# Stream products of an attention step in 32-column weight blocks, and the stream values by token rows

## What is computed

```python
def dsa_attend(q, qi, wi, k_all, v_all, ki_all, q_pos, k_pos, top_k):
    s_idx = jnp.einsum('bthd,bsd->bths', qi, ki_all)
    score = jnp.einsum('bths,bth->bts', jax.nn.relu(s_idx), wi) * IDX_SCALE
    score = jnp.where(adm[None], score, NEG)          # chunk-causal
    _, idx = lax.top_k(score, top_k)
    ...
    logits = jnp.einsum('bthd,btkhd->bhtk', q, k_sel) * (HEAD_DIM ** -0.5)
    p = jax.nn.softmax(jnp.where(valid[:, None], logits, NEG), axis=-1)
    return jnp.einsum('bhtk,btkhd->bthd', p, v_sel)
```

## Time and profile before

| | |
|---|---|
| Time, median of 3 runs | 2992.81 us (2989.2 to 2993.98) |
| The profiled execution's own time | 2993.22 us |
| Its span, first to last instruction | 2991.4 us |
| TensorE matmul busy | 2916.6 us, 97% |
| TensorE weight load busy | 2874.6 us, 96% |
| VectorE, ScalarE, GpSimd busy | 46%, 34%, 33% |
| DMA | 238.8 MB, 80 GB/s |
| Mean granted TensorE clock | 0.987 of full speed |

### The profile page before, as it was taken

The page is one execution under the profiler, slowest core; times in us unless marked ns, Lnnn a source line. Parts: engine busy times, 40 slices in busy tenths (PEclk is TensorE's granted clock), DMA queues, the critical chain, the costliest instruction groups (busy, mean ns, idle before and its releaser), DMA issues.

```text
span 2991.4 us, 50397 instructions
## 1 busy us (share of the span) xinstructions
PE 2916.6 (97%) x19500; PEld 2874.6 (96%) x19516; DVE 1361.3 (46%) x1857; ACT 1012.5 (34%) x1431; POOL 997.1 (33%) x468
## 2 busy tenths in 40 slices
PE   8999999999999999999999999999989999999997
PEld 8999999988899999999999999999889999999997
DVE  4324246777533532424532333568674334324245
ACT  5312225536432342212343222254463323412223
POOL 2333333241233333333333333333312333333332
PEclk9999999999999999999999999999999999999998
DMA  3222222232122222222222222222321222222222
GB/s 116 77 78 70 84 77 85 77 116 92 59 70 77 71 77 75 73 84 71 84 71 73 75 77 77 79 84 84 117 86 59 77 74 74 70 78 77 77 77 91
DMA packets 73073, 238.80 MB, mean 80 GB/s; under 512 B 8336, under 2 KB 16784, under 8 KB 72464
## 3 DMA queue, kind: packets, MB, share of 16 engines
q1 hardware_dynamic: 58464, 210.00, 20.6%
q10 hardware_dynamic: 14512, 27.51, 2.6%
HBM read 229.22 MB, written 8.27 MB: 79 GB/s over the span
## 4 chain that ended last, share of the span: by engine, by line
issue 58%; PE 26%; POOL 13%; POOLq 1%; DVE 1%; ACT 1%; ACTq 0%; DVEq 0%
PE lin L404 22%; POOL w_lo L339 12%; PE bank L404 2%; POOLq L379 0%; POOL tmp L370 0%; PE bank L565 0%; PE bank L550 0%; POOLq L337 0%; POOL tmp L376 0%; PE lin L565 0%; PE bank L527 0%; POOLq L392 0%; PE lin L527 0%; DVE x L1479 0%; PE bank L575 0%
## 5 line engine op out<-in xcount | busy, mean ns | idle before, releaser
L339 POOL TENSOR_TENSOR w_lo<-w_raw,w_hi 128x1024 fp32r<-128x1024 f32 x392 | 948.3, 2419 | 1951.7 <-ACT w_hi L706 1940.2
L404 PE MATMUL lin<-h_hi,w_hi 128*128 128x320 f32 x4064 | 939.6, 313 | 18.8 <-DVE h_lo L1048 12.1
L404 PE MATMUL lin<-h_lo,w_hi 128*128 128x320 f32 x4064 | 931.3, 311 | 0.0
L404 PE MATMUL lin<-h_hi,w_lo 128*128 128x320 f32 x4064 | 930.5, 310 | 0.0
L706 ACT ACTIVATE w_hi<-w_raw 128x1024 fp32r<-128x1024 f32 x392 | 415.4, 1060 | 1508.0 <-PE lin L404 1380.6
L404 PEld LDWEIGHTS lin<-h_hi,w_hi 128*128 128x128 f32 x4064 | 684.2, 189 | 25.9 <-DVE h_lo L1048 12.9
L404 PEld LDWEIGHTS lin<-h_lo,w_hi 128*128 128x128 f32 x4064 | 683.8, 189 | 0.0
L404 PEld LDWEIGHTS lin<-h_hi,w_lo 128*128 128x128 f32 x4064 | 683.5, 189 | 0.0
L404 PE MATMUL lin<-g_lo,w_hi 128*128 128x320 f32 x1408 | 321.2, 309 | 0.0
L404 PE MATMUL lin<-g_hi,w_hi 128*128 128x320 f32 x1408 | 321.1, 309 | 0.0
L404 PE MATMUL lin<-g_hi,w_lo 128*128 128x320 f32 x1408 | 321.1, 309 | 0.0
(11 more groups left out here) (211 smaller groups left out, 2550.5 us busy)
## 6 DMA issues: line engine op xcount, KB each, us to landing
w_raw<-wts SPq DMA_DIRECT2D x394, 512.0 KB, 3.2
caches<-kcache_in ACTq DMA_DIRECT2D x16, 512.0 KB, 3.8
caches<-vcache_in ACTq DMA_DIRECT2D x16, 512.0 KB, 4.4
x<-x_in SPq DMA_DIRECT2D x8, 320.0 KB, 6.6
k_out<-kT ACTq DMA_DIRECT2D x2, 1280.0 KB, 8.6
v_out<-v_sb ACTq DMA_DIRECT2D x2, 1280.0 KB, 11.7
y_out<-x ACTq DMA_DIRECT2D x8, 320.0 KB, 2.4
ki_cache<-kidx_in ACTq DMA_DIRECT2D x2, 512.0 KB, 3.3
```

What stands on the lines that cost most here:

```text
L339: nc.gpsimd.tensor_tensor(w_lo[:, s, :], w_raw[:, s, :], w_hi[:, s, :].bitcast(F), ALU.subtract).then_inc(lo_ready.sem, 1)
L404: ins = nc.tensor.matmul(out[:, half, :], w, a[:, half * HALF:(half + 1) * HALF], start=first and n == 0, stop=last and n == 2)
```

## The change

The streams' weights are cut to the 32 columns that hold anything, and each of the four blocks writes its own 32 partitions of the PSUM bank.

- `qi_diag` and `q_diag` shrink from four 128x128 matrices per buffer to one, in which block `c` (or pair) holds columns 32c to 32c+31. Line 509 becomes four separate products, each starting and ending its own sum on partitions 32c to 32c+31; line 527's four products add to the mask's rows on those partitions. Moving columns (256 and 272) and the count of products stay.
- In `weigh`, weight and moving operand of a stream change places: the weight is 32 columns of `pT_s`, moving are 128 value columns, and the result has the token and head on the partitions. The loop order becomes key block outside, `c` inside. There are still 12 float32 products.
- The values' result is turned back. ScalarE copies the 128x128 result out of the bank (`take_rows`, at the start of its step u+4), TensorE transposes it into columns 128 to 255 of the same bank (`turn_rows`, at the end of its step u+4), and VectorE's `keep_out` of a stream reads from there, one step later than before, after `pT_lo` of step u+5.
- The two memsets shrink from 1024 to 256 columns.

```diff
@@ -156,8 +156,10 @@
         r, _ = new("r", [P, T])
         sq, sq_at = new("sq", [P, T])
         acc, _ = new("acc", [P, T])
-        q_diag = at("q_diag", [P, 2, AB, P], F, sq_at)
-        v_lo_part = at("v_lo_part", [P, 2, P], F, sq_at + 4 * 2 * AB * P)
+        q_diag = at("q_diag", [P, 2, P], F, sq_at)
+        v_lo_part = at("v_lo_part", [P, 2, P], F, sq_at + 4 * 2 * P)
+        o_rows = at("o_rows", [P, P], F, sq_at + 4 * 4 * P)
+        assert 5 * P <= T
 
 
         cache_words = AB * KEYS + 2 * ATT_W
@@ -168,8 +170,8 @@
         scores = at("scores", [P, 9 * P], F, cache_at)
         s_scores = at("s_scores", [P, SLOTS], F, cache_at + 4 * 9 * P)
         ki_cache = at("ki_cache", [P, 4, PAST], F, cache_at + 4 * cache_words)
-        qi_diag = at("qi_diag", [P, 2, 4, P], F, cache_at + 4 * cache_words + 16 * PAST)
-        assert 9 * P + SLOTS <= cache_words and 4 * PAST + 8 * P <= cache_words
+        qi_diag = at("qi_diag", [P, 2, P], F, cache_at + 4 * cache_words + 16 * PAST)
+        assert 9 * P + SLOTS <= cache_words and 4 * PAST + 2 * P <= cache_words
         tmp, _ = new("tmp", [P, 3, T])
         prob, prob_at = new("prob", [P, 2, 4 * P])
         bmask_f = at("bmask_f", [P, P], F, prob_at)
@@ -292,6 +294,8 @@
         pT_split = Signal("pT_split", 4 * HEADS)
         pv_done = Signal("pv_done", NU)
         v_lo_out = Signal("v_lo_out", 2 * HEADS)
+        o_rows_out = Signal("o_rows_out", STREAMS)
+        o_rows_turned = Signal("o_rows_turned", STREAMS)
         o_summed = Signal("o_summed", 2 * HEADS)
         o_kept = Signal("o_kept", NG)
         o_att_hi = Signal("o_att_hi", AB)
@@ -506,8 +510,9 @@
                 else:
                     pe.wait_ge(qi_placed.sem, qi_placed.count(L, h + 1))
                     for pair in range(4):
-                        nc.tensor.matmul(out[:, 0:PAST], qi_diag[:, h % 2, pair, :], ki_cache[:, pair, :],
-                                         start=pair == 0, stop=pair == 3)
+                        cols = slice(32 * pair, 32 * pair + 32)
+                        nc.tensor.matmul(out[cols, 0:PAST], qi_diag[:, h % 2, cols], ki_cache[:, pair, :],
+                                         start=True, stop=True)
                     nc.tensor.matmul(out[:, PAST:PAST + P], rows, ki_hi[:, SEQ:T], start=True, stop=False)
                     ins = nc.tensor.matmul(out[:, PAST:PAST + P], rows, ki_lo[:, SEQ:T], start=False, stop=True)
                 ins.then_inc(idx_products.sem, 1)
@@ -523,9 +528,9 @@
                     rows = spread[:, a % 2, :, :].rearrange("p h t -> p (h t)")
                     nc.tensor.matmul(out[:, 0:KEYS], rows, s_mask[:, :], start=True, stop=False)
                     for c in range(AB):
-                        w = q_diag[:, a % 2, c, :]
-                        ins = nc.tensor.matmul(out[:, 0:KEYS], w, k_cache[(a + 1) % 2][:, c, :],
-                                               start=False, stop=c == AB - 1)
+                        cols = slice(32 * c, 32 * c + 32)
+                        ins = nc.tensor.matmul(out[cols, 0:KEYS], q_diag[:, a % 2, cols],
+                                               k_cache[(a + 1) % 2][:, c, :], start=False, stop=True)
                 else:
                     n = unit_columns(u)
                     if a == 0:
@@ -558,12 +563,12 @@
                     pe.wait_ge(o_kept.sem, o_kept.count(L, g - 1))
                 if kind == "stream":
                     pe.wait_ge(pT_hi.sem, pT_hi.count(L, u + 1))
-                    for c in range(AB):
-                        for b in range(nb):
+                    for b in range(nb):
+                        for c in range(AB):
                             v = (v_cache[(a + 1) % 2][:, b * ATT_W + c * P:b * ATT_W + (c + 1) * P] if b < 2
                                  else v_sb[:, TT - 1, c * P:(c + 1) * P])
-                            ins = nc.tensor.matmul(out[:, c * 32:(c + 1) * 32], v,
-                                                   pT_s[:, b * P + c * 32:b * P + (c + 1) * 32],
+                            ins = nc.tensor.matmul(out[c * 32:(c + 1) * 32, 0:P],
+                                                   pT_s[:, b * P + c * 32:b * P + (c + 1) * 32], v,
                                                    start=b == 0, stop=b == nb - 1)
                 else:
                     if a == 0:
@@ -576,6 +581,13 @@
                                                pT[k % 2][:, b, :, :].rearrange("p two q -> p (two q)"),
                                                start=b == 0, stop=b == nb - 1)
                 ins.then_inc(pv_done.sem, 1)
+
+            def turn_rows(L, u):
+
+                b = ATT_UNITS[u][1]
+                pe.wait_ge(o_rows_out.sem, o_rows_out.count(L, b + 1))
+                nc.tensor.transpose(out_banks[GROUP_OF[u] % 2][:, P:2 * P], o_rows[:, :],
+                                    ident[:, :]).then_inc(o_rows_turned.sem, 1)
 
             pe.wait_ge(ones_set, 1)
             with pe.Fori(0, DEPTH) as L:
@@ -657,6 +669,8 @@
                         weigh(L, step - 3)
                     for tile, c in PIECES[step] if new_tile else []:
                         piece(tile, c)
+                    if step >= 4 and ATT_UNITS[step - 4][0] == "stream":
+                        turn_rows(L, step - 4)
 
                 with pe.Fori(0, KB // 2) as jj:
 
@@ -766,9 +780,8 @@
                 src = qiT[64 * (h % 2):64 * (h % 2) + 64, h // 2, SEQ:T].rearrange(
                     "p (pair par t) -> p pair par t", pair=4, par=2)
                 for par in range(2):
-                    dst = qi_diag[64 * par:64 * par + 64, h % 2, :, :].rearrange(
-                        "p pair n -> p (pair n)")
-                    dst = diagonal(dst, 16 * par, P + 2 * NEW, 4)
+                    dst = qi_diag[64 * par:64 * par + 64, h % 2, :].rearrange(
+                        "p (pair two t) -> p pair two t", pair=4, two=2)[:, :, par, :]
                     ins = nc.scalar.activation(dst, src[:, :, par, :], ACT.Copy)
                 ins.then_inc(qi_placed.sem, 1)
 
@@ -781,8 +794,8 @@
                 if b >= 2:
                     act.wait_ge(logits_done.sem, logits_done.count(L, 5 * (b - 2) + 1))
                 for par in range(2):
-                    dst = q_diag[64 * par:64 * par + 64, b % 2, :, :].rearrange("p c n -> p (c n)")
-                    dst = diagonal(dst, 16 * par, P + 2 * NEW, AB)
+                    dst = q_diag[64 * par:64 * par + 64, b % 2, :].rearrange(
+                        "p (c two t) -> p c two t", c=AB, two=2)[:, :, par, :]
                     src = qT[64 * par:64 * par + 64, :, SEQ + NEW * b:SEQ + NEW * (b + 1)]
                     nc.scalar.activation(dst, src, ACT.Copy)
 
@@ -847,6 +860,15 @@
                 src = out_banks[GROUP_OF[u] % 2].rearrange("p (a two q) -> p a two q", a=2, two=2)
                 nc.scalar.activation(v_lo_part[mine:mine + 64, :, :], src[other:other + 64, :, 0, :],
                                      ACT.Copy).then_inc(v_lo_out.sem, 1)
+
+            def take_rows(L, u):
+
+                b = ATT_UNITS[u][1]
+                act.wait_ge(pv_done.sem, pv_done.count(L, u + 1))
+                if b:
+                    act.wait_ge(o_rows_turned.sem, o_rows_turned.count(L, b))
+                nc.scalar.activation(o_rows[:, :], out_banks[GROUP_OF[u] % 2][:, 0:P],
+                                     ACT.Copy).then_inc(o_rows_out.sem, 1)
 
             act.dma_start(gains[:, :], gains_in).then_inc(gains_landed, 16)
             def first_split(s):
@@ -976,6 +998,8 @@
                 for step in range(NU + 4):
                     if step - 4 in LAST_OF and ATT_UNITS[step - 4][0] == "prompt":
                         take_v_lo(L, step - 4)
+                    if 0 <= step - 4 < NU and ATT_UNITS[step - 4][0] == "stream":
+                        take_rows(L, step - 4)
                     if 0 <= step - 2 < NU:
                         take_turned(L, step - 2)
                     if step < NU:
@@ -1230,15 +1254,16 @@
 
                 kind, a, h = ATT_UNITS[u]
                 g = GROUP_OF[u]
-                dve.wait_ge(pv_done.sem, pv_done.count(L, u + 1))
                 if kind == "stream":
-                    o = out_banks[g % 2][:, 0:P].rearrange("p (c n) -> p c n", c=AB)
+                    dve.wait_ge(o_rows_turned.sem, o_rows_turned.count(L, a + 1))
+                    o = out_banks[g % 2][:, P:2 * P].rearrange("p (c n) -> p c n", c=AB)
                     for par in range(2):
                         lane = slice(64 * par, 64 * par + 64)
                         ins = nc.vector.tensor_copy(qT[lane, :, SEQ + NEW * a:SEQ + NEW * (a + 1)],
                                                     o[lane, :, NEW * par:NEW * (par + 1)])
                 else:
                     k = 2 * h + a // 2
+                    dve.wait_ge(pv_done.sem, pv_done.count(L, u + 1))
                     lane = slice(64 * (h % 2), 64 * (h % 2) + 64)
```

(13 more changed lines are left out.)

## The result

| | before | changed |
|---|---|---|
| Time, median | 2991.63 us of 4 (2989.2 to 2993.98) | 2945.19 us of 4 (2943.3 to 2945.88) |
| The profiled execution's own time, and its span | 2993.22, 2991.4 | 2943.3, 2941.5 |
| TensorE matmul, weight load busy | 2916.6, 2874.6 | 2858.4, 2799.3 |
| Mean granted TensorE clock | 0.987 | 0.991 |

The ratio is 0.9844, with a 95% interval of 0.9827 to 0.9861. The forecast was 2971 us in a range of 2942 to 3000, with the direction right and less than half of the gain. The time is that of the second rival, all four blocks at once, 2946 us.

What follows compares the result with a forecast made beforehand. Attention was taken as bound by TensorE, with some hand-over stalls. Sections 19.8 us less 1.6 for copies gave 18.2; half-clock values 2 and clock 2 made 22, so 2993.2 - 22 = 2971 us, range 2942 to 3000.

Steps and rivals of the forecast that it cites:

- second rival: Stream sections on TensorE: all four blocks run at once, 47 us gained, 2946 us; chance 0.18.
- order of issue: Stream float32 matmuls: passes start in order, so eight take 5 slots and 24 take 13.
- moved copies: VectorE's two copies of a stream's values, moved behind pT_lo of the next step: 0.1 us per stream lost, 1.6 us.
- first rival: Stream sections: only a block's second pass runs beside the next block's first; 2971 us, chance 0.45.
- Switches: TensorE going to 32-column weights and back: 0.15 us each, 0.30 a section, 12 us for all 40.
- The transpose: TensorE turning a stream's values result back, at the end of step u+4: 0.11 us each.
- third rival: Stream sections: no overlap between blocks, so the kernel gets slower, 3009 us; chance 0.15.
- Does it arrive?: Whether section savings reach the kernel's time: waits leave room for 0.38 (logits), 0.69 (values) and 0.34 us (index).
- the text's own test: Transposes' waits for pT growing from 15.7 us by over 8 would show the hand-over as the bound.
- fifth rival: Hand-over through the probability split becomes the bound, half the gain goes into waits: 2982 us; chance 0.15.
- Clock: TensorE clock: three value sections at half clock gain 2 us more, another 2 us added, +-8 in the range.
- fourth rival: Quarter-array sections make the TensorE clock fall after streams that keep it today; all 16 give 3003 us; chance 0.07.

Runs made afterwards that it cites:

- logits_64: Kernel before with the logits' weights cut to 64 columns, two blocks on each half of the rows: 2983.32 us, ratio 0.9974.
- values_by_block: Changed kernel with the values' two loops exchanged back, six passes of one strip in a row: 2950.14 us, ratio 0.9858 to the kernel before.
- same_tile: Changed kernel with all narrow logits, index and values products written to the first 32 rows of their bank: 2989.68 us, ratio 0.9993 to the kernel before.
- rows_mid: Changed kernel with the values' rows transposed behind the turn of the step and the qT copies back in their old step: 2944.2 us, ratio 0.9842.
- logits_only: Kernel before with only the logits' products cut to 32 weight columns on four strips: 2977.12 us, ratio 0.9947.
- index_only: Kernel before with only the index products' weights cut to 32 columns on four strips: 2984.61 us, ratio 0.9973.
- values_only: Changed kernel with logits and index products put back to 128 weight columns: 2967.03 us, ratio 0.9919 to the kernel before.
- mask_tiled: Changed kernel with the mask's one product cut into four of 32 weight columns on four strips: 2947.88 us, ratio 0.9847 to the kernel before.

## Why the forecast was right or wrong, step by step

**The step that failed** is the order of issue, from which the number of slots in the sum was taken: "if passes start in order, only the second pass of block c can run beside the first of block c+1". What the runs fit is that passes are handed out in order, but a strip takes up to four of them before it has worked them off, so the first pass of block c+1 doesn't wait for the second of block c. With two or four in a row all four strips run at once: 2 slots for the logits in place of 5, 2 for the index in place of 5, 6 for the values in place of 13. Of the three terms, the sections' times were to be 1.15, 1.08 and 1.50 us besides the switches; they are 0.46, 0.42 and 0.65. Of the sum, the sections at full clock brought 49.8 us where 19.8 were counted.

That the time is the second rival's 2946 is in part luck. Its 47 us price the values by weight loading, cap the logits at 0.94 and leave out the clock, the waits and the 1.6 for the moved copies; measured are 49.8 from the sections, 10 from the clock and 8 given back. (With the switch at 0.05 to 0.25 the first rival's sum gives 2963 to 2979, not 2962 to 2981.)

The Trainium skill (TensorE: Matmul & The Clock Gate, Part 3) gave 2.38 times for three column tiles and says that matmuls start and end in program order. The first agrees in kind with the 8 passes in 2 slots here. The second cannot hold pass by pass: in logits_64 the passes one to four are for one half and five to eight for the other, and all eight need four slots (the rows start in pairs 0.01 us apart, and a half's passes are 0.23 apart), so the fifth ran beside the first, ahead of the second. The Trainium skill (TensorEngine Tiling (Array Packing), Key Properties) calls the tiles independent in loading and multiplying; values_by_block, at 1.52 us in place of 0.8, shows the limit of that.

**Switches.** 0.30 a section, forecast; measured 0.14 for entering and 0.18, 0.12 and 0.20 for leaving behind logits, values and index. Right, and the same with no overlap at all (1.95 and 2.74 us in same_tile).

**The transpose** 0.11: right. **No overlap** (the third rival): same_tile is this case. Its sections are as worked out there, but the time is 2989.7, not 3009; section times add 16 x 0.30 + 16 x 0.37 + 8 x 0.32 = 13 us to the kernel before, the time at half clock, 48.2 us in place of 74.6, takes 13 off (below), and TensorE's idle time, 70.9 in place of 74.4, takes 3 or 4.

**Does it arrive?** Mostly. The rule that a matmul microsecond counts held to 8 us in 50: TensorE's idle time rose from 74.4 to 82.6. In the text's own test, waits for `pT` growing by over 8 us from 15.7, they grew by 7.2: the fifth rival is there as a cost of 8 us, not as the outcome. After a stream's logits VectorE no longer waits at all, where it waited 0.49:

```profile
695.01 0.42 DVE L1297 TENSOR_TENSOR v_both<-v_sb,v_both 128x256 fp32r<-128x256 f32 x1
695.34 0.44 DVE L1232 TENSOR_REDUCE neg_max<-bank 128x1 f32<-128x272 f32 x1
```

so logits that are faster still would bring the row maximum no earlier here. **The moved copies**, 1.6 us: rows_mid puts them back (and turns the rows earlier) and is 2 us faster than the changed kernel beside it, within the intervals; neither confirmed nor excluded.

**Clock.** Forecast were 2 us for value sections at half clock and 2 us of gain, with 8 either way. Time at half clock, from windows of 1 us as above: in the four kernels whose values stayed dense 74.6 (before), 76.4 (logits_only), 74.5 (index_only) and 64.2 (logits_64), in the mean 72.4; in the twelve executions with the values by rows between 44.6 (values_only) and 72.0 (mask_tiled), in the mean 57.7. The difference of 15 us is worth 7 us of time. The scatter in the second group is as large as the difference, and two executions of the same changed kernel had 54.7 and 61.5. So a gain is likely, its size is not settled, and what in the value sections brings it wasn't isolated. The falls still follow stalls, as in the earlier trace rows; here a stall of 3.00 us stands before values at half clock, which take 1.21 us (749.28 to 750.49) in place of 0.79:

```profile
748.95 0.33 PE L555 MATMUL bank<-ident,prob 128*128 128x128 f32 x1 [3.00 <-DVE prob L1251]
749.21 0.86 PE L570 MATMUL bank<-caches,pT_s 128*32 128x128 f32 x16
749.82 0.67 PE L570 MATMUL bank<-v_sb,pT_s 128*32 128x128 f32 x8
```

The fourth rival's sign, many more stretches at half clock, did not come: each of the two traces has eleven, the last one at the end of the span, and none after is longer than 6.8 us ahead of it, where before three are 10.2.

## What to carry to other kernels

Where several products use only 32 weight columns each, giving each its own strip of PSUM partitions runs four of them in the time of one, at some 0.3 us per block of such work for going in and out (1.3 of these passes of 272 columns). Lay them out strip by strip in turn, with no more than four passes (two float32 products) of one strip in a row. Then look at the hand-over: the shorter the matmul sections, the more of the gain ends as waits on the other engines, here 8 us of 50.

## What the runs showed of the hardware that was not expected

- Strips of 32 rows run four at once also in float32, whose products are two passes: 8 passes of 272 columns in 0.46 us and 24 of 128 in 0.65; halves of 64 run two at once, 8 passes in 0.94.
- A strip holds about four passes, the one at work among them, and the next for it stops all others: the same 32 passes of 68 columns take 1.39 us with eight in a row and 0.61 with two; 24 of 128 columns take 1.52 with six in a row and 0.81 with four.
- Going to 32-column weights costs 0.14 us and back 0.12 to 0.20, the same whether anything overlaps.
- A pass of 32-column weights on one strip lasts as long as its columns: 0.229 us for 272, no less than with 128 columns of weights. But where dense weights move 32 columns, a pass took 0.11, and 32 narrow loads fit into 0.47 us, 0.015 each.
